# Moving the tokens of seven experts by indirect DMA through HBM instead of one-hot matmuls

## The reference, cut to what matters

```python
def moe_swiglu(x, router_w, router_b, w1, w3, w2):
    logits = (x @ router_w + router_b).astype(jnp.float32)
    top_v, top_i = lax.top_k(logits, TOP_K)
    top_p = jax.nn.softmax(top_v, axis=-1)
    gate = jnp.sum(jax.nn.one_hot(top_i, N_EXPERTS, dtype=jnp.float32) * top_p[..., None], axis=-2)
    gate = gate.astype(x.dtype)
    out = jnp.zeros_like(x)
    for e in range(N_EXPERTS):
        out = out + gate[..., e:e + 1] * swiglu(x, w1[e], w3[e], w2[e])
    return out
```

## Time and profile before

| | us |
|---|---|
| median of 3 runs | 2210.69 (2207.57 to 2210.99) |
| the profiled execution | 2203.56 |
| its span, first to last instruction | 2201.6 |
| mixture of experts, first wave to last down product | 716.8 to 1438.7 |
| PE busy over the span | 2131.2 (97%) |
| DVE, ACT, POOL busy | 746.1, 430.4, 0.2 |
| moved by DMA | 524.39 MB, mean 238 GB/s |

### The profile page before, as it was taken

How to read it: one execution, slowest core, us unless ns; L and a number is a source line. 1 busy time by engine, 2 the same in 40 slices (tenths; PEclk the granted TensorE clock), 3 DMA queues, 4 the chain that set the end, 5 groups by cost and what they waited for, 6 DMA issues and landing times.

```text
span 2201.6 us, 28675 instructions
## 1 busy us (share of the span) xinstructions
PE 2131.2 (97%) x12059; PEld 1227.1 (56%) x12059; DVE 746.1 (34%) x1529; ACT 430.4 (20%) x969; POOL 0.2 (0%) x4
## 2 busy tenths in 40 slices
PE   8988999999977999999999999999999999999998
PEld 5664777765754533333333323365677776667775
DVE  2563476323763100110110101035546743831112
ACT  2464000132463000000000001052410002420001
POOL 0000000000000000000000000000000000000000
PEclk9999999999989999999999999999999999999999
DMA  6222995233302999889999999723487651383230
GB/s 229 104 92 88 424 349 198 110 124 141 118 20 113 424 389 395 342 355 424 400 414 421 370 426 402 297 108 133 183 333 289 221 219 58 127 342 120 82 124 19
DMA packets 58340, 524.39 MB, mean 238 GB/s; under 512 B 8544, under 2 KB 9056, under 8 KB 20320
## 3 DMA queue, kind: packets, MB, share of 16 engines
q1 hardware_dynamic: 48992, 472.19, 53.1%
q10 hardware_dynamic: 9216, 50.34, 6.3%
HBM read 521.44 MB, written 1.06 MB: 237 GB/s over the span
## 4 chain that ended last, share of the span: by engine, by line
PE 88%; DVE 7%; ACT 3%; issue 1%; DMA 0%; DVEq 0%; ACTq 0%; SPq 0%
PE ps L90 88%; DVE ring L90 5%; ACT ring L90 2%; DVE stat L90 1%; ACT L90 1%; DVE natural L90 0%; DVE transposed L90 0%; DVE residual L90 0%; DVE gates L90 0%; ACT natural L90 0%; DVE z L90 0%; DMA residual<-in_x 0%; ACT z L90 0%; ACT transposed L90 0%; ACT gates L90 0%
## 5 line engine op out<-in xcount | busy, mean ns | idle before, releaser
L90 PE MATMUL ps<-ring 128*32 128x512 f32 (+10 forms) x3784 | 532.8, 517 | 15.7 <-ACT ring L90 6.3
L90 PE MATMUL ps<-ring,z 128*32 128x512 f32 (+3 forms) x2048 | 477.1, 586 | 2.1 <-ACT ring L90 1.2
L90 PE MATMUL ps<-ring,transposed 128*128 128x384 f32 (+4 forms) x1408 | 471.4, 491 | 3.1 <-DVE transposed L90 2.4
L90 PE MATMUL ps<-transposed,ring 128*128 128x257 f32 (+2 forms) x2128 | 470.2, 379 | 1.3 <-DVE transposed L90 1.3
L90 PEld LDWEIGHTS ps<-transposed,ring 128*128 128x128 f32 (+1 forms) x2128 | 399.8, 189 | 85.5 <-issue 30.4
L90 PEld LDWEIGHTS ps<-ring,transposed 128*128 128x128 f32 x1408 | 260.7, 191 | 186.5 <-issue 62.5
L90 PEld LDWEIGHTS ps<-ring 128*32 128x32 f32 (+4 forms) x3784 | 196.0, 129 | 297.6 <-issue 270.4
L90 PEld LDWEIGHTS ps<-ring,z 128*32 128x32 f32 (+2 forms) x2048 | 173.6, 140 | 250.8 <-issue 239.3
L90 DVE TENSOR_TENSOR z<-z,ps 128x256 f32<-128x256 f32 (+4 forms) x94 | 38.9, 414 | 547.1 <-ACT z L90 526.5
L90 ACT COPY z<-ps 128x256 f32<-128x256 f32 (+5 forms) x121 | 48.3, 399 | 511.9 <-PE ps L90 511.0
L90 ACT ACTIVATE z<-ps 128x256 f32<-128x256 f32 (+2 forms) x87 | 32.6, 374 | 443.2 <-PE ps L90 233.3
(11 more groups left out here) (138 smaller groups left out, 1029.6 us busy)
## 6 DMA issues: line engine op xcount, KB each, us to landing
ring<-in_moe SPq DMA_DIRECT2D x87, 2048.0 KB, 13.3
ring<-in_ffn SPq DMA_DIRECT2D x66, 1536.0 KB, 9.8
ring<-in_moe SPq DMA_DIRECT2D x90, 1024.0 KB, 12.0
ring<-in_w_in SPq DMA_DIRECT2D x25, 1536.0 KB, 6.4
z<-in_ada ACTq DMA_DIRECT2D x48, 768.0 KB, 5.3
ring<-in_w_out SPq DMA_DIRECT2D x12, 1536.0 KB, 7.4
natural<-in_ada ACTq DMA_DIRECT2D x16, 768.0 KB, 5.9
ring<-in_ple_gate SPq DMA_DIRECT2D x4, 1536.0 KB, 6.2
```

The lines of the kernel that those rows point to most:

```text
L90: self.ins = None if self.book.counting else op(*args, **kw)
```

## The change

Seven experts' results, and six experts' inputs, no longer go through PE's one-hot matmuls.

- DVE works out two row numbers for each token, one per chosen expert (`dve_rows`). POOL sends the 256 normalized tokens twice, by 4 indirect DMAs of 128 rows of 4 KB, to a scratch `sent` in HBM, where each expert's rows lie together. SP has zeroed those rows before, from an input of zeros (`sp_zero_rows`).
- For experts 1, 2, 3, 4, 6 and 7, POOL loads the expert's rows back into a half of `xn` (`pool_rows`), and PE turns them by 8 transposes (`pe_mo_turn_rows`) in place of the 16 matmuls. Experts 0 and 5 (`PICKED`) keep the gather.
- The gates and scatter tasks stay for expert 4 alone. The output of each other expert is stored by POOL to a scratch `made` (`pool_store`), after DVE has added the two halves that the third block of 32 tokens has in PSUM (`dve_mo_y`).
- When all are stored, POOL fetches for each token its first and then its second expert's row, by 2 + 2 indirect DMAs, and DVE adds them to `h`, weighted by the gate, after waves 60 and 62 (`dve_rows_add`). A token whose expert is the last fetches a row of zeros for it.
- POOL takes part in the branch.

The tasks left, by wave: gather 5 at 0, 1 at 12, 6 at 15, 2 at 25, 7 at 33, 3 at 38, 4 at 51; gates 4 at 57.

```diff
-WORKERS = (EngineType.PE, EngineType.Activation, EngineType.DVE)
+WORKERS = (EngineType.PE, EngineType.Activation, EngineType.DVE, EngineType.Pool)
+LAST = 4
+ROW_AT = tuple(1 + sum(CAP[y] for y in range(NE) if y != LAST and (y < x or x == LAST)) for x in range(NE))
...
+    def move_rows(self, dst, dst_rows, src, src_rows, into, signal):
...
+            self.q.indirect_dma_start(dst, by(dst_rows), src, by(src_rows)).then_inc(self.book.sem(key), 16)
...
+    PICKED = (LANES[0][0], LANES[1][0])
+    BY_ROWS = [x for x in sorted(range(NE), key=lambda x: FIRST_WAVE[x]) if x not in PICKED]
...
             start = FIRST_WAVE[before(x)] if before(x) is not None else 0
+            if x not in PICKED:
+                start = max(start, FIRST_WAVE[x] - 5)
             waiting.append((2 * FIRST_WAVE[x] - 1, 2 * start, ("gather", x, 0), None))
-        for x in range(NE):
-            b = before(x)
-            waiting.append((2 * LAST_WAVE[x] + 2, 2 * FIRST_WAVE[x] + 2, ("gates", x, 0), None if b is None else ("scatter", b, 1)))
-            if x != LANES[0][-1]:
-                waiting += [(2 * LAST_WAVE[x] + 16, 2 * LAST_WAVE[x] + 5, ("scatter", x, i), ("gates", x, 0)) for i in range(NT)]
+        waiting.append((2 * LAST_WAVE[LAST] + 2, 2 * FIRST_WAVE[LAST] + 2, ("gates", LAST, 0), None))
...
+    sent = nc.dram_tensor("tokens_sent", (ROW_AT[LAST] + CAP[LAST], D), F32, kind="Internal").ap()
+    made = nc.dram_tensor("tokens_made", (ROW_AT[LAST], D), F32, kind="Internal").ap()
 
     def expert_tokens(x, k):
         return mo_xg[lane(x)][:, turn_in_lane(x) % 2, k * CAP[x]:(k + 1) * CAP[x]]
...
+    def rows_at(x):
+        return xn[:, BY_ROWS.index(x) % 2, :]
+    def pe_mo_turn_rows(x):
+        pe.wait_ge(f"mo.rows{x}")
+        n = CAP[x]
+        for half in range(2):
+            for k in range(4):
+                at = (4 * half + k) * P
+                pe(T.transpose, ps[:, gather_banks(x)[half], k * n:(k + 1) * n], rows_at(x)[0:n, at:at + P], C("ident")[0:n, 0:n])
+            pe.then_inc(f"mo.gather{x}{half}")
+    def dve_rows():
+        by_token = lambda t: t.rearrange("p e i -> p i e")
+        dve(V.tensor_scalar, rx_chosen, ro_pos, 0.0, None, ALU.is_ge)
+        dve(V.tensor_tensor, rx_row, ro_pos, spread(C("base"), 2, NT), ALU.add)
+        dve(V.tensor_tensor, rx_row, rx_row, rx_chosen, ALU.mult)
+        dve(V.tensor_reduce, rx_of[:, 0:2], by_token(rx_row), AXX, ALU.max)
+        dve(V.tensor_reduce, rx_of[:, 2:4], by_token(rx_row), AXX, ALU.add)
+        dve(V.tensor_tensor, rx_of[:, 2:4], rx_of[:, 2:4], rx_of[:, 0:2], ALU.subtract)
+        dve(V.tensor_copy, row_i[:, 0:4], rx_of).then_inc("rows.sent")
+    def dve_rows_back():
+        by_token = lambda t: t.rearrange("p e i -> p i e")
+        dve(V.memset, rx_row[:, LAST, :], 0.0)
+        dve(V.memset, rx_chosen[:, LAST, :], 0.0)
+        dve(V.tensor_reduce, rx_of[:, 0:2], by_token(rx_row), AXX, ALU.max)
+        dve(V.tensor_reduce, rx_of[:, 2:4], by_token(rx_row), AXX, ALU.add)
+        dve(V.tensor_tensor, rx_of[:, 2:4], rx_of[:, 2:4], rx_of[:, 0:2], ALU.subtract)
+        dve(V.tensor_copy, row_i[:, 4:8], rx_of).then_inc("rows.back")
+        dve(V.tensor_tensor, rx_first, rx_row, spread(rx_of[:, 0:2], 1, NE), ALU.is_equal)
+        dve(V.tensor_tensor, rx_first, rx_first, ro_gate, ALU.mult)
+        dve(V.tensor_tensor, rx_chosen, rx_chosen, ro_gate, ALU.mult)
+        dve(V.tensor_reduce, rx_gate[:, 0, :], by_token(rx_first), AXX, ALU.add)
+        dve(V.tensor_reduce, rx_gate[:, 1, :], by_token(rx_chosen), AXX, ALU.add)
+        dve(V.tensor_tensor, rx_gate[:, 1, :], rx_gate[:, 1, :], rx_gate[:, 0, :], ALU.subtract)
+    def dve_rows_add(c):
+        for i in range(NT):
+            dve.wait_ge(f"rows.made{c}{i}")
+            dve(V.scalar_tensor_tensor, out=h[:, i, :], in0=xn[:, i, :], scalar=rx_gate[:, c, i:i + 1], in1=h[:, i, :],
+                op0=ALU.mult, op1=ALU.add).then_inc(f"rows.added{c}{i}")
+    def pool_send():
+        pool.wait_ge("rows.sent", "ffn1.natural0", "ffn1.natural1", "sent.zero")
+        for c in range(2):
+            for i in range(NT):
+                pool.move_rows(sent, row_i[:, 2 * c + i:2 * c + i + 1], xn[:, i, :], None, "sent", f"rows.sent{c}{i}")
+    def pool_rows(x):
+        n, at = CAP[x], ROW_AT[x]
+        k = BY_ROWS.index(x)
+        if k < 2:
+            pool.wait_ge("rows.sent11", *(f"mo.gather{y}1" for y in PICKED))
+        else:
+            pool.wait_ge(f"mo.gather{BY_ROWS[k - 2]}1")
+        pool.load(rows_at(x)[0:n, :], sent[at:at + n, :], f"rows{k % 2}", f"mo.rows{x}")
+    def pool_store(x):
+        y, at = mo_y[lane(x)], ROW_AT[x]
+        pool.wait_ge(f"mo.y{x}.sum" if CAP[x] == 96 else f"mo.y{x}")
+        if CAP[x] == P:
+            pool.load(made[at:at + P, :], y.rearrange("p b n -> p (b n)"), f"made{lane(x)}", f"mo.stored{x}")
+            return
+        for q in range(2):
+            cols_ = slice(q * 512, (q + 1) * 512)
+            if CAP[x] == 96:
+                pool.load(made[at + 64:at + 96, cols_], y[64 * q:64 * q + 32, 1, :], f"made{lane(x)}", f"mo.stored{x}.high{q}")
+            pool.load(made[at:at + 64, cols_], y[64 * q:64 * q + 64, 0, :], f"made{lane(x)}", f"mo.stored{x}" if q else f"mo.stored{x}.first")
+    def pool_back(c):
+        if c == 0:
+            pool.wait_ge("rows.back", "made.zero", *(f"mo.gather{x}1" for x in BY_ROWS[-2:]),
+                         *(f"mo.stored{x}" for x in range(NE) if x != LAST))
+        for i in range(NT):
+            if c:
+                pool.wait_ge(f"rows.added0{i}")
+            pool.move_rows(xn[:, i, :], None, made, row_i[:, 4 + 2 * c + i:5 + 2 * c + i], f"back{i}", f"rows.made{c}{i}")
+    def pool_gathered():
+        pool_send()
+        done = [(0, 0, x) for x in BY_ROWS[0:2]]
+        done += [(FIRST_WAVE[BY_ROWS[k]] - 1, 0, BY_ROWS[k + 2]) for k in range(len(BY_ROWS) - 2)]
+        done += [(LAST_WAVE[x] + 1, 1, x) for x in range(NE) if x != LAST]
+        for _, kind, x in sorted(done):
+            if kind:
+                pool_store(x)
+            else:
+                pool_rows(x)
+        pool_back(0)
+        pool_back(1)
+    def sp_zero_rows():
+        for x in BY_ROWS:
+            at = ROW_AT[x]
+            sp.load(sent[at:at + CAP[x], :], d["zeros"][0:CAP[x], :], "sent_zero", "sent.zero" if x == BY_ROWS[-1] else f"sent.zero{x}")
+        sp.load(made[0:1, :], d["zeros"][0:1, :], "made_zero", "made.zero")
     def pe_mo_gather(x):
+        if x not in PICKED:
+            pe_mo_turn_rows(x)
+            return
         pe.wait_ge(f"mo.pick{x}")
         if x == 0:
...
-        if before(x) is not None:
-            act.wait_ge(f"mo.scatter{before(x)}1")
...
-    def dve_mo_add(x, i):
...
-                pe_mo_scatter(x, n)
...
-            pe.wait_ge("ple1.kept1" if before(x) is None else f"mo.y{before(x)}")
+            b = before(x)
+            pe.wait_ge("ple1.kept1" if b is None else f"mo.y{b}.sum" if CAP[b] == 96 else f"mo.y{b}")
...
         if before(x) is not None:
-            act.wait_ge(f"mo.scatter{before(x)}1")
-        for b in range(1 if x == LAST else out_banks(x)):
+            act.wait_ge(f"mo.stored{before(x)}")
+        for b in range(1 if CAP[x] == 96 else out_banks(x)):
             act(S.copy, mo_y[lane(x)][:, b, :], ps[:, (2, 5)[lane(x)] + b, :])
+        if CAP[x] == 96 and x != LAST:
+            for at in (0, 64):
+                act(S.copy, mo_y[lane(x)][at:at + 32, 1, :], ps[at + 32:at + 64, 3, :])
...
+    def dve_mo_y(x):
...
+        dve.wait_ge(f"mo.y{x}")
+        for at in (0, 64):
+            y = mo_y[lane(x)][at:at + 32, 1, :]
+            dve(V.tensor_tensor, y, y, ps[at:at + 32, 3, :], ALU.add)
+        dve.then_inc(f"mo.y{x}.sum")
...
+    ADD_AFTER = (FIRST_WAVE[LAST] + 4, FIRST_WAVE[LAST] + 6)
     def dve_gathered():
         dve_mo_aux(-1)
+        dve_rows()
         for g in range(len(WAVES)):
             dve_mo_aux(2 * g)
             dve_mo_hid(g)
+            for x in range(NE):
+                if CAP[x] == 96 and x != LAST and g == LAST_WAVE[x] + 1:
+                    dve_mo_y(x)
+            if g == 1:
+                dve_rows_back()
+            if g in ADD_AFTER:
+                dve_rows_add(ADD_AFTER.index(g))
             dve_mo_aux(2 * g + 1)
...
         sp_mixers1(1, after)
+        sp_zero_rows()
         sp_ple_up(1, PLE1_UP_SLOT, slots_after_mixers1(1))
...
+        pool_gathered()
```

More of the change, by code:

```diff
@@ L114, in load @@
             self.q.dma_start(dst, src, **kw).then_inc(self.book.sem(key), 16)
+    def move_rows(self, dst, dst_rows, src, src_rows, into, signal):
+        self.close()
+        key = f"landed_{into}"
+        n = self.count[key] = self.count.get(key, 0) + 16
+        by = lambda rows: None if rows is None else bass.IndirectOffsetOnAxis(rows, 0)
+        if self.book.counting:
+            self.book.value[signal] = (key, n)
+        else:
```

(38 more changed lines are left out.)

3 lines of the change are left out of this document (added).

## The result

| | before | after |
|---|---|---|
| median | 2209.13 us, 4 runs (2205.88 to 2210.99) | 2183.43 us, 4 runs (2180.84 to 2186.46) |
| the profiled execution | 2203.56 | 2180.84 |
| its span | 2201.6 | 2179.3 |
| first wave to the end of the last wave's matmuls | 718.7 | 695.8 |

The account below looks back on a forecast made before the run. PE was taken to bound the expert stage, with weight loads right behind it. PE work removed -46.4, transposes +6.6, weight waits +4.6, start +0.3 make -34.9 us: 2210.7 to 2175.8 us, range 2167 to 2199.

Parts of the forecast that it names:

- main case: Whole kernel: PE's turn cost between its bounds, the branch, 0 to 10 us lost to weights; 2168 to 2184, chance 0.6.
- PE's work: Expert stage: gathers, scatters and gates removed, 46.4 us, less 6.6 added for transposes; net 39.8 us less.
- The turns: Six experts' rows, 8 transposes each on PE: 1.1 us per expert, 6.6 us added (5.4 to 14.4).
- Loss to weights: 960 to 1300 us: 19.7 us asked of the DMA engines, 13.6 unused, 1.5 lead; 4.6 us of gain lost.
- The place: Weight waits expected near waves 47 to 52; no loss taken from 900 to 960 us or after wave 52.
- The size near 47 to 52: Waits for weights near waves 47 to 52, 4.6 us, from one sum over 960 to 1300 us.
- The price of a byte: Row traffic of 8.8 MB at 425 GB/s: 20.7 us of all 16 DMA engines.
- The start: Wave 2: sends take 4.9 us, the weights' lead falls from 8.5 to about -0.3; 0.3 us lost.
- A: Row traffic costs weights far more than its bytes: 2201 us, milder form at twice its bytes 2188; chance 0.2.
- B: First waves: all four sends queue on one DMA engine, 74 us lost, 2250 us, slower than before; chance 0.05.
- C: After wave 60: fetched rows come late, DVE and PE stand; a 60 us fetch gives 2196 us; chance 0.05.
- D: No change, as weights bind the whole expert stage: 2208 us; chance 0.05.

Follow-up runs that it names:

- the run without bytes: The changed kernel with every POOL row transfer cut to 16 columns (64 bytes) of a row, 0.14 MB in all; 2171.78 us.
- outputs alone: The changed kernel with all eight inputs back at the one-hot gather and nothing sent; only outputs go through HBM; 2185.13 us.

## Why the prediction was right, and where its gain went

The time, 2183.43, lies in the range and at the upper edge of the forecast's main case, 2168 to 2184. That case allowed 0 to 10 us lost to weights, and 17.6 were lost. So the mechanism named, PE first and the weights right behind it, is the one that the runs show, but the size of the loss was wrong, and that the time still falls into the main case is in part luck: PE lost 2 us more work than forecast, and the medians gained 3.0 us more than the profiled executions.

**PE's work: right.** The stage from the first wave to the end of the last is 22.9 us shorter (718.7 to 695.8). With 12.5 us of waits, 5.1 behind them, and 1.2 at the start given back, the work that PE lost is 41.7 us; the run without bytes gives 34.3 + 6.7 + 0.9 = 41.9 by the same count. The forecast had 39.8. The turns make up the 2 us between: 6.6 forecast, 4.7 measured as busy time and 4.2 from start to start, below its lower bound of 5.4.

**Loss to weights: the term that was mis-sized.** 4.6 us were forecast, 17.6 came. Four things were wrong with it.
- *The place.* The forecast said: "From 900 to 960 us the engines move only 312 GB/s, with the ring full ... I take no loss there." That step failed. PE waits 2.64 us in wave 22, at 958. The room was real: 39 / 425 x 120 = 11.0 us from 780 to 900, 113 / 425 x 60 = 16.0 to 960, 1.3 more to wave 22, together 28.3. But it was never set against what would be asked up to that wave. In the run without bytes, PE reaches wave 22 237.9 us after the stage's start (720.04 to 957.90), against 256.7 before (716.84 to 973.55): 18.8 sooner. By then POOL has moved 4.2 MB (the sends, rows of 1, 6, 2 and 7, stores of 0 and 5), which at 2.7 us per MB is 11.3. Together 30.1. The room was gone before the stretch for which I did the sum. This account is an estimate. Before, the load for wave 22 landed at 971.13, 2.4 us ahead, so by the account 0.6 us were still to spare where PE waited 2.64; it is good to some 3 us. That the rows used up the room is shown by the runs: without their bytes the same load is 1.2 us ahead and PE does not wait.
- *The size near 47 to 52.* The waits are there, in waves 47 and 48, with 1.7 + 3.6 + 1.7 us. Of these the run without bytes keeps 5.3. I had set the room of 960 to 1300 us against the work of the whole stretch; it also had to be enough up to wave 48, for waits are settled wave by wave. Wave 38 (3.4 us in after; without bytes none there, and 1.4 in wave 39) was missed in this way. The sum itself has a slip: four turns lie between 960 and 1300 us (experts 2, 7, 3 and 4, at 995, 1077, 1134 and 1278 in after), not three. At the forecast's price that would have made the loss smaller, 3.5 us, so it does not explain the miss.
- *The price of a byte.* The rows took 23.7 us of the engines in place of 20.7.
- *The price of a wait.* Of the 17.6 us, 5.1 are clock lost behind long waits, for which the sum had no term.

The forecast said "none of more than 2 us elsewhere" than waves 47 to 52, and that was wrong twice, in waves 22 and 38.

**The start: right in effect.** No wait in waves 1 to 6, against A and B. The sends took 16.4 us each to landing, POOL's next load waited 21.0 us for all four, and the lead of the up part of piece 3, 8.5 before, was still 3.9 (landed at 737.54, used at 741.39). The tightest there is a later piece, which landed at 773.88 and is used at 774.02, in wave 5, without a gap in PE's work. The 1.2 us at the start are the first half of wave 0: 6.26 us from its beginning to the gather behind it (717.51 to 723.77), 5.03 before (716.84 to 721.87). PE stood idle ahead of it in both kernels, and begins at a granted clock of 0.50 in both; from 717.5 to 724 us it is 0.57 in after, from 717 to 722 us it is 0.71 before. The 0.97 from 720 to 780 us goes with it. The sends are not the reason: the first is issued at 723.49, the half wave is as slow with the sends 45 us later, and it still takes 1.0 us more than before in the run that sends nothing (outputs alone). What is the reason stays open.

**The rivals.** A in its mild form, "all row traffic at twice its bytes, loses another 10 to 15: 2188", named the right direction: the rows cost 10.6 us. Its reason was wrong, as the engines carry them at 1.15 times the time forecast. They are dear because the engines had no room left for them: of some 16 us that the 6.0 MB moved before wave 48 take of the engines (at 2.7 us per MB, an estimate), 10.6 were lost by PE. B did not come. C did not: the fetched rows landed 12.4 us after issue, and DVE waited for none. D, that weights bind the whole stage, is half true, which the forecast did not allow for. Up to wave 48 the engines have a share of 1.01 throughout and PE waits in five waves; behind it, from 1241 us, PE works 172 us without a wait at a DMA share of 0.94 from 1300 on. The Trainium skill's rule that an engine alternates between queues ("DMA: Bandwidth & Descriptors", "Queues, rings and completion order") was said to move when weights are late and not by how much; the late weights in waves 22 and 38, gone with the bytes, are in line with it, and no run here tests it.

**The signs.** The chain ends at 1413.3, where near 1404 was named. 421 GB/s from 960 to 1300 us against 418 or more: right, and of no use as a sign, since it does not say whether PE waits.

The executions also differ ahead of the stage: it starts at 717.5 us in after and at 718.1 to 722.9 us in the experiments. So lengths of the stage are compared here, not its ends.

## What to carry to other kernels

When a resource stands close behind the one that binds, work out its account at every point where it can be late, from the last point at which it had caught up, and not over a stretch: room that lies in a quiet stretch is spent by what is asked before and in it. Two changes that each give their full price can share the same room, so time them together and not only apart. Once a second resource has become the bound up to some point, more work taken from the first ahead of that point brings little: here 11.4 us of matmuls, exchanged for 1.3 MB of rows that the second had to carry, were worth 1.5 to 4 us.

## What the runs showed of the hardware

- Of 19 waits of PE of 2.6 to 4.1 us in these traces, 18 were followed by half a wave in 5.06 to 5.35 us in place of 3.64; where the window was read, at a granted clock of 0.70, part of it at 1.2 GHz. After waits of up to 2.04 us nothing was lost. Of three waits of 2.3 to 2.5 us one was followed by the loss and two were not. The one exception, a wait of 3.71 us in the run with sends and stores written twice, cost nothing behind it (granted clock 1.00 over the 5.6 us that follow), and why is open.
- Small row transfers are not fast beside a full queue of loads: stores of 2 KB took 6.1 us to landing (in the run with hardly any bytes), stores of 128 KB 7.2, indirect sends of 0.52 MB 16.4. The Trainium skill, "DMA: Bandwidth & Descriptors", section "Anatomy of one DMA — SWDGE (gpsimd) path", gives 2.0 us plus the bytes at 436 GB/s for one, an estimate of 3.2 us for a send. The trace does not agree where the engines are at a share of 1.01.
- Indirect sends are cheap to issue, 0.95 to 1.12 us each on POOL:

```profile
723.49 1.12 POOL L127 DMA_INDIRECT tokens_sent<-natural,row_numbers  x1 [723.03 <-DVE row_numbers L92]
724.91 0.96 POOL L127 DMA_INDIRECT tokens_sent<-natural,row_numbers  x1 [0.30 <-issue]
```
